# Norm totals from three matmuls, and ACT work moved inside a recurrence: one change to a five-engine transformer kernel

## The chip, the cores and the metric

One Trainium2 chip, one of its cores. The time is device microseconds of one execution. Before the change three runs took 2352.44, 2352.53 and 2354.01 us; their median is 2352.53 us. The engines are named as in the profile: PE (TensorE: matmuls and transposes, into PSUM), PEld (its weight loads), ACT (ScalarE), DVE (VectorE), POOL (GpSimd) and SP (SyncE, which issues the DMAs here).

## The reference

The kernel computes two transformer blocks on 512 tokens of width 1024, all in fp32. The first block has two layers, each an attention and an FFN with a short convolution; the second mixes a window attention, a global attention and a two-way gated recurrence over 64-wide heads, merges the three through sigmoid gates, and ends in an FFN and a norm. What the change touches is the norm, the recurrence's inputs and the merge:

```
def rmsnorm(x, g):
    y = x32 * lax.rsqrt(jnp.mean(x32 * x32, axis=-1, keepdims=True) + RMS_EPS)
    return (y * g)                       # before each attention and FFN
# second block, features of the recurrence: q and g pass through silu
# merge: sum over the three branches of sigmoid(gate) * (branch @ w_branch), then @ w_out
```

## The kernel before

**Layout.** x is held transposed in SBUF, 8 tiles `XT` of 128 features by 512 tokens. Features lie on partitions, so the mean of squares over features is a sum over partitions and over tiles.

**Weights.** Every 128 output columns of a weight matrix are a unit. Its weights come by DMA into `raw`; ACT copies them as fp32r, their high part, into `wH` (L460); DVE subtracts and leaves the low part in `wL` (L465). PE then does three matmuls for each 128 input features: high by high (L478), low by high (L479), high by low (L480), 512 tokens each. A ring of three `raw`, `wH` and `wL` buffers lets the conversion of a unit run ahead of PE; the conversion three units ahead is queued behind the eviction of the unit now done.

**Order of work.** There are five programs, one for each engine, and each is a fixed list. Signals (semaphores) tie them. An engine that waits holds up all that stands behind it on its list.

**Norm totals.** For a norm ACT squares tile k into `sq[k % 2]` (tile 0 straight into `ssum`; `ac_square`, L520), and one lane adds it to `ssum` (`add_square`, L527): DVE in the first attention ("attn0"), POOL in all others ("attn1", "ffn0", "ffn1", "ctx", "end1"). When all eight are in, PE multiplies `ssum` by a matrix of ones in plain fp32 (`pe_total`, L531, into PSUM bank 7), which sums over partitions, and ACT makes the factor with Ln and Exp (`ac_scale`). After the FFN of layer 1 two norms are needed at once, that of the block's end and the next block's; the second works on squares with a gain, `ssum_g`, and its own bank 6 (`pe_end_sums`, `pe_last_sums`). There the POOL sum runs to tile 6, and tile 7 comes in by a second matmul on each bank.

**The recurrence.** `g_order` (L2273) writes one list of items, and each engine's program takes from it what is its own. "ticks" are steps of the projection units that fill PE between the recurrence's own matmuls; their results are evicted by ACT (L2384), and the next gate's unit may wait for that. For each of four heads the items d (DVE, L2716 and L2718) and x (ACT, L2660) make the decay factors, w the products (DVE, L2730), use the score matmuls (PE, L2591), cp the masking (DVE, L2745), out the head's output. yh and yl split the branch outputs into high and low parts (`ac_split` on ACT, L2471, and `ve_split` on DVE, L2475) for the merge. silu is two Silu activations on ACT between two table loads (L2614 to L2617).

**The merge.** For each of 24 pairs of tile and branch, PE multiplies the branch output by its weights, ACT has a sigmoid of the gate ready (`ac_sigmoid`, L2482), DVE multiplies the two (L2878). In the order of the merge, ACT and DVE also do the last four splits (8 to 11).

Of the kernel before, what the change touches and what calls it, by code (L numbers as in the profile page):

```python
# [148 lines left out]
def build_in(nc, t, out, ctx):  # L149
# [551 lines left out]
    def ve_begin(ve):  # L701
# [11 lines left out]
        for k in range(1, KD):  # L713
            add_square(ve, ss_v, "attn0", k, S)
# [167 lines left out]
    def ve_fill(ve, layer):  # L882
        for x in fill[layer]:
# [15 lines left out]
            elif x.kind in ("q", "k"):  # L899
# [11 lines left out]
                if layer and x.kind == "k" and x.u == 1:  # L911
                    ve_factor(ve, 1)
# [615 lines left out]
    def pe_ffn(pe, layer):  # L1528
# [5 lines left out]
        for half in range(2):  # L1534
            for j in range(HALF):
                n = half * HALF + j
                for what, u, b in (("v", n, j % 2), ("g", 22 + n, 2 + j % 2)):
# [94 lines left out]
    def ac_ffn(ac, layer):  # L1632
# [18 lines left out]
        for half in range(2):  # L1651
# [40 lines left out]
            for m in range(8):  # L1692
# [8 lines left out]
                if half == 1:  # L1701
                    ac.wait_ge(*x_s.at(((down, 1), m)))
                    if layer == 1:
# [26 lines left out]
    def ve_ffn(ve, layer, scale=None):  # L1730
# [3 lines left out]
        if layer < 2:  # L1734
            ffn_free(ve, layer)
            if layer == 1:
                ve.do.tensor_tensor(sc1[:, 57:58], M("final", 7, 8), M("final", 7, 8), ALU.mult).then_inc(*gain_e.up(0))
                ve.wait_ge(*gain_e.at(0))
                ve.do.tensor_scalar(sc1[:, 57:58], sc1[:, 57:58], EPS, None, ALU.add).then_inc(*gain_e.up(1))
# [156 lines left out]
    def ffn1_done(lane):  # L1896
# [376 lines left out]
    def g_order():  # L2273

        out_ = [("ticks", 0, 2), ("sc", 0, 0), ("fa", 0, 1), ("fb", 0, 0), ("ticks", 0, 2), ("fv", 0, 1), ("sc", 0, 1),
                ("silu", 0), ("ke", 0, 0), ("kd", 0, 0), ("fb", 0, 1), ("ke", 0, 1), ("kd", 0, 1), ("ticks", 0, 4), ("v6", 0),
                ("ticks", 0, 99)]
        for h in range(4):
# [15 lines left out]
            out_ += [("use", h, 1), ("cp", h, 0), ("d", h, 4), ("w", h, 3), ("state", h, 1), *split(0), ticks_(3, 3), ("x", h, 4), ticks_(1, 1)]  # L2294
            out_ += [("use", h, 2), ("cp", h, 1), ("w", h, 4), ("d", h, 5), ("qe", h), *split(1), ticks_(1, 3), ("x", h, 5), ticks_(1, 1)]
            out_ += [("use", h, 3), ("cp", h, 2), ("w", h, 5), ("d", h, 6), *split(2), ticks_(2, 3), ("x", h, 6), ticks_(1, 1)]
            out_ += [("use", h, 4), ("cp", h, 3), ("w", h, 6), ("d", h, 7), ("qa", h), *split(3), ticks_(2, 3), ("x", h, 7), ticks_(1, 1)]
            out_ += [("use", h, 5), ("cp", h, 4), ("w", h, 7), *opens(("fa", 0)), *split(4), ticks_(2, 4)]
            out_ += [("use", h, 6), ("cp", h, 5), *opens(("fv", 0), ("fa", 1), ("sc", 0)), ticks_(3, 3)]
            out_ += [("use", h, 7), ("cp", h, 6), *opens(("fb", 0), ("ke", 0), ("kd", 0)), *split(5), ticks_(2, 2), ("cp", h, 7), ticks_(1, 1)]  # L2300
            out_ += [*opens(("fv", 1)), ("out", h), ("o", h), *opens(("sc", 1)), *split(6, 7), ticks_(3, 2)]
# [905 lines left out]
```

## Time and profile before

| | |
|---|---|
| median of three runs | 2352.53 us |
| the profiled execution | 2354.01 us |
| its span (first to last instruction) | 2352.2 us |
| PE busy | 2321.8 us (99%) |
| PEld busy | 1866.4 us (79%) |
| DVE busy | 1422.9 us (60%) |
| ACT busy | 1088.8 us (46%) |
| POOL busy | 407.4 us (17%) |
| fp32 sum matmuls L531 | 5 |
| POOL additions of squares L527, mean | 1470 ns |

The busy share of an engine is a mean over the whole span. In a timeline a row starts at its first number; the second is its length, and starts of consecutive matmuls stand closer than their lengths, because they are pipelined. Idle time before an instruction, where the profile shows it, stands in brackets with what ended it.

### The profile page before, as it was taken

The numbers are of one execution on the slowest core, as the hardware profiler recorded it, in microseconds if no ns is written. First come the engines' busy times: TensorE is split into PE (matmuls) and PEld (weight loads), VectorE is DVE, ScalarE is ACT, GpSimd is POOL, SyncE is SP. The second block draws the span as 40 slices with busy tenths as digits, with TensorE's granted clock in tenths as the row PEclk, the third lists the DMA queues.
The fourth block names the chain that finished last, engine by engine and source line by source line (L and its number), as shares of the span: only waits on it lengthen the run. The fifth ranks groups of instructions, "written<-read, shape, count | busy, mean of one in ns | idle before, by whom it ended". The sixth has DMA issues, their size and how long they took to land.

```text
span 2352.2 us, 30161 instructions
## 1 busy us (share of the span) xinstructions
PE 2321.8 (99%) x11870; PEld 1866.4 (79%) x11870; DVE 1422.9 (60%) x2280; ACT 1088.8 (46%) x1772; POOL 407.4 (17%) x304
## 2 busy tenths in 40 slices
PE   9999999999999999999999999999999999999998
PEld 7567678888887777888888878778887889888887
DVE  5887568858654546674676475557777335543443
ACT  4455654424435445442444356675555324432442
POOL 0001322202210001221122130012222222220222
PEclk9999999999999999999999999999999999999999
DMA  5222143433423222444342221011111432232331
GB/s 178 65 88 77 54 157 130 153 120 126 145 88 108 73 68 94 170 157 136 102 161 99 92 83 69 16 48 55 54 50 45 134 117 85 99 110 87 99 110 61
DMA packets 69933, 233.03 MB, mean 99 GB/s; under 512 B 8000, under 2 KB 10176, under 8 KB 69536
## 3 DMA queue, kind: packets, MB, share of 16 engines
q1 hardware_dynamic: 69792, 231.11, 29.3%
q8 instruction: 94, 1.54, 0.3%
q14 instruction: 47, 0.39, 0.0%
HBM read 224.18 MB, written 4.28 MB: 97 GB/s over the span
## 4 chain that ended last, share of the span: by engine, by line
PE 63%; DVE 4%; ACT 2%; issue 1%; DMA 0%; POOL 0%; DVEq 0%; SPq 0%; ACTq 0%
PE psum L478 17%; PE psum L479 17%; PE psum L480 17%; PE psum L1097 1%; PE psum L1122 1%; PE psum L1141 1%; PE psum L2011 1%; PE psum L2012 1%; PE psum L2013 1%; PE psum L1272 1%; PE psum L1283 1%; PE psum L1295 1%; DVE wL L465 1%; PE psum L2591 1%; DVE X L2716 0%
## 5 line engine op out<-in xcount | busy, mean ns | idle before, releaser
L478 PE MATMUL psum<-hH,wH 128*128 128x512 f32 (+1 forms) x1904 | 765.5, 402 | 11.5 <-ACT zc L2400 3.3
L480 PE MATMUL psum<-hH,wL 128*128 128x512 f32 (+1 forms) x1904 | 741.8, 390 | 0.0
L479 PE MATMUL psum<-hL,wH 128*128 128x512 f32 (+1 forms) x1904 | 740.6, 389 | 0.0
L465 DVE TENSOR_TENSOR wL<-raw,wH 128x1024 fp32r<-128x1024 f32 (+2 forms) x353 | 447.5, 1268 | 358.0 <-ACT wH L460 356.2
L460 ACT ACTIVATE wH<-raw 128x1024 fp32r<-128x1024 f32 (+2 forms) x353 | 363.3, 1030 | 481.1 <-PE psum L480 479.7
L478 PEld LDWEIGHTS psum<-hH,wH 128*128 128x128 f32 x1904 | 358.7, 188 | 115.8 <-issue 37.8
L480 PEld LDWEIGHTS psum<-hH,wL 128*128 128x128 f32 x1904 | 358.5, 188 | 75.0
L479 PEld LDWEIGHTS psum<-hL,wH 128*128 128x128 f32 x1904 | 359.3, 189 | 62.4 <-issue 0.7
L1845 POOL TENSOR_TENSOR sg<-sg,cv 128x512 f32<-128x512 f32 x66 | 95.1, 1441 | 676.9 <-ACT sg L1674 676.9
L478 PE MATMUL psum<-gH,wH 128*128 128x512 f32 x506 | 197.5, 390 | 0.0
L480 PE MATMUL psum<-gH,wL 128*128 128x512 f32 x506 | 196.9, 389 | 0.0
L479 PE MATMUL psum<-gL,wH 128*128 128x512 f32 x506 | 196.8, 389 | 0.0
L527 POOL TENSOR_TENSOR ssum<-ssum,sq 128x512 f32<-128x512 f32 (+1 forms) x44 | 64.7, 1470 | 401.3 <-ACT sq L520 400.2
L1310 ACT ACTIVATE Pr<-Sp,mn 128x128 f32<-128x128 f32 (+3 forms) x128 | 70.9, 555 | 101.4 <-DVE mn L1347 101.3
L1446 DVE TENSOR_TENSOR XT<-psum,XT 128x512 f32<-128x512 f32 x64 | 44.1, 689 | 118.3 <-PE psum L480 118.3
L478 PEld LDWEIGHTS psum<-gH,wH 128*128 128x128 f32 x506 | 95.0, 188 | 20.0 <-issue 0.2
L479 PEld LDWEIGHTS psum<-gL,wH 128*128 128x128 f32 x506 | 95.0, 188 | 19.8 <-issue 0.2
L480 PEld LDWEIGHTS psum<-gH,wL 128*128 128x128 f32 x506 | 95.0, 188 | 19.8
L1674 ACT ACTIVATE sg<-cg 128x512 f32<-128x512 f32 x66 | 41.8, 633 | 132.7 <-DVE cg L1772 132.7
L1847 POOL TENSOR_TENSOR gL<-sg,gH 128x512 fp32r<-128x512 f32 x66 | 87.9, 1332 | 49.0 <-ACT gH L1678 49.0
L1678 ACT ACTIVATE gH<-sg 128x512 fp32r<-128x512 f32 x66 | 41.7, 632 | 102.8 <-POOL sg L1845 102.8
L1763 DVE TENSOR_TENSOR hf<-psum,rs 128x512 f32<-128x512 f32 x88 | 60.5, 687 | 41.8 <-PE psum L480 25.9
(379 smaller groups left out, 3357.8 us busy)
## 6 DMA issues: line engine op xcount, KB each, us to landing
raw<-in_up SPq DMA_DIRECT2D x132, 512.0 KB, 3.6
raw<-in_dn SPq DMA_DIRECT2D x48, 704.0 KB, 4.0
raw<-in_win SPq DMA_DIRECT2D x56, 512.0 KB, 3.6
mbuf<-in_wmod SPq DMA_DIRECT2D x48, 512.0 KB, 3.7
raw<-in_we SPq DMA_DIRECT2D x33, 512.0 KB, 3.7
raw<-in_wq SPq DMA_DIRECT2D x24, 512.0 KB, 3.6
tm<-toep SPq DMA_DIRECT2D x32, 256.0 KB, 4.3
raw<-in_wo SPq DMA_DIRECT2D x32, 256.0 KB, 2.6
```

The source lines that it names most:

```text
L460: ac.do.activation(flat_of(wHb, n), flat_of(rawb, n), ACT.Copy).then_inc(*w_hi.up(n))
L465: ve.do.tensor_tensor(flat_of(wLb, n), flat_of(rawb, n), flat_of(wHb, n).bitcast(F), ALU.subtract).then_inc(*w_lo.up(n))
L478: pe.do.matmul(o, H[:, k, :], high(k), start=k == 0, stop=False)
L479: pe.do.matmul(o, H[:, k, :], low(k), start=False, stop=False)
L480: ins = pe.do.matmul(o, L[:, k, :], high(k), start=False, stop=k == kt - 1)
L527: lane.do.tensor_tensor(ssum[:, :n], ssum[:, :n], sq[k % 2][:, :n], ALU.add).then_inc(*own.up((z, k)))
L1310: ac.do.activation(Pr[:, s % 2, u, :W], Sp[:, u, :W], ACT.Exp, scale=-1.0, bias=mn[:, h:h + 1, i], accum_out=den[:, h:h + 1, i]).then_inc( ...
L1446: ve.do.tensor_tensor(xt(m), b, xt(m), ALU.add).then_inc(*x_s.up((key, m)))
L1674: ac.do.activation(sg[q][:], cg_[q][:], ACT.Silu).then_inc(*sg_a.up((layer, n)))
L1763: ve.do.tensor_tensor(of_[:], bank[b], rs[:], ALU.mult).then_inc(*up_s.up((layer, n, what)))
L1845: po.do.tensor_tensor(sg[q][:], sg[q][:], cv[q][:], ALU.mult).then_inc(*sg_p.up((layer, n)))
L1847: po.do.tensor_tensor(gL[:, j, :], sg[q][:], gH[:, j, :].bitcast(F), ALU.subtract).then_inc(*gl_s.up((layer, half, j)))
```

## The change

**Norm sums.** The additions of squares stop at tile 5. PE's total is now three fp32 matmuls that accumulate in bank 7: of `ssum`, of `sq[0]` (tile 6) and of `sq[1]` (tile 7). POOL does nine additions fewer (two each in ffn0, attn1, ffn1 and ctx, one in end1), DVE two fewer (attn0). The total of ffn0 and of ffn1 moves ahead by one unit, that of attn1 by six matmuls.

```
     def pe_total(pe, z, n):
-        pe.wait_ge(*(ss_v if z == "attn0" else ss_p).at((z, KD - 1)))
-        pe.do.matmul(bank[7][:, :n], C("ones"), ssum[:, :n], start=True, stop=True).then_inc(*tot.up(z))
+        pe.wait_ge(*(ss_v if z == "attn0" else ss_p).at((z, 5)))
+        pe.do.matmul(bank[7][:, :n], C("ones"), ssum[:, :n], start=True, stop=False)
+        pe.wait_ge(*sq_s.at((z, 6)))
+        pe.do.matmul(bank[7][:, :n], C("ones"), sq[0][:, :n], start=False, stop=False)
+        pe.wait_ge(*sq_s.at((z, 7)))
+        pe.do.matmul(bank[7][:, :n], C("ones"), sq[1][:, :n], start=False, stop=True).then_inc(*tot.up(z))
...
-                if i == 1 and layer and x.u == 1:
+                if i == 7 and layer and x.u == 0:
                     pe_total(pe, "attn1", S)
-                if i == 2 and layer and x.u == 2:
+                if i == 7 and layer and x.u == 1:
                     pe_factor(pe, 1)
...
-        last = {"ffn2": 5, "final": 5, "end1": 6}.get(z, KD - 1)
-        if 1 <= m <= last:
+        if 1 <= m <= 5:
             add_square(po, ss_p, z, m, n)
...
-                    if layer < 2 and n == 0 and what == "g":
+                    if layer < 2 and n == 0 and what == "v":
                         pe_total(pe, z, S)
```

In PE's list at ffn0 the total stands, before, between the unit on `wH_57` and that on `wH_55` (`cn` holds the ones):

```order
L478 MATMUL psum<-hH,wH_57 128x512
L479 MATMUL psum<-hL,wH_57 128x512
L480 MATMUL psum<-hH,wL_60 128x512
L478 MATMUL psum<-hH,wH_57 128x512
L479 MATMUL psum<-hL,wH_57 128x512
L480 MATMUL psum<-hH,wL_60 128x512
L531 MATMUL psum<-ssum,cn 128x512
L478 MATMUL psum<-hH,wH_55 128x512
```

and in the changed kernel:

```order
L478 MATMUL psum<-hH,wH_56 128x512
L479 MATMUL psum<-hL,wH_56 128x512
L480 MATMUL psum<-hH,wL_59 128x512
L478 MATMUL psum<-hH,wH_56 128x512
L479 MATMUL psum<-hL,wH_56 128x512
L480 MATMUL psum<-hH,wL_59 128x512
L531 MATMUL psum<-ssum,cn 128x512
L533 MATMUL psum<-sq_65,cn 128x512
L535 MATMUL psum<-sq_66,cn 128x512
L478 MATMUL psum<-hH,wH_57 128x512
```

One instruction has become three, and they stand one unit of 24 matmuls earlier, ahead of the unit on `wH_57`.

**End of the first block.** One matmul more on each bank, one DVE operation replaced by another, and two squares on ACT for tile 7, one of them scaled by the root of epsilon into a new buffer `sq_eps`:

```
         pe.wait_ge(*rs_ln.at("ctx"))
-        pe.wait_ge(*ss_p.at(("end1", 6)))
+        pe.wait_ge(*ss_p.at(("end1", 5)))
         pe.do.matmul(bank[7], C("ones"), ssum[:], start=True, stop=False)
+        pe.wait_ge(*sq_s.at(("end1", 6)))
+        pe.do.matmul(bank[7], C("ones"), sq[0][:], start=False, stop=False)
         pe.wait_ge(*x_s.at((("dn1", 1), 5)))
-        pe.wait_ge(*sgv.at("sum"))
+        pe.wait_ge(*sgv.at("eps"))
         pe.do.matmul(bank[6], C("ones"), ssum_g[:], start=True, stop=False)
 
     def pe_last_sums(pe):
-        pe.wait_ge(*sgv.at("last"))
-        pe.do.matmul(bank[6], C("ones"), hf[0][:], start=False, stop=True).then_inc(*rr_mm.up(0))
+        pe.wait_ge(*sg2.at(7))
+        pe.do.matmul(bank[6], C("ones"), hf[0][:], start=False, stop=False)
+        pe.wait_ge(*sg2.at("eps"))
+        pe.do.matmul(bank[6], C("ones"), sq_eps[:], start=False, stop=True).then_inc(*rr_mm.up(0))
...
-                elif half == 1 and layer == 1 and m == 7:
-
-                    ve.wait_ge(*x_s.at(((down, 1), 7)))
-                    ve.wait_ge(*gain_e.at(1))
-                    ve.do.scalar_tensor_tensor(hf[0][:], xt(7), sc1[:, 57:58], xt(7), ALU.mult, ALU.mult).then_inc(*sgv.up("last"))
+                    ve.wait_ge(*sgv.at("sum"))
+                    ve.wait_ge(*sq_s.at(("end1", 6)))
+                    ve.do.scalar_tensor_tensor(ssum_g[:], sq[0][:], EPS, ssum_g[:], ALU.mult, ALU.add).then_inc(*sgv.up("eps"))
```

**The opening of the recurrence.** The item ("silu", 0) moves behind the two key items and four ticks. ACT's list right behind the conversion into `wH_57`, before (`kd`, `kcc` and `f` are key products and decays; `XT<-psum` is the eviction of a gate's unit):

```order
L2615 ACT_TABLE_LOAD
L2615 ACTIVATE qt_129<-qt_129 128x512
L2616 ACTIVATE yc<-yc 128x512
L2617 ACT_TABLE_LOAD
L2537 ACTIVATE kd_152<-PS 128x256
L2541 ACTIVATE kd_152<-PS 128x128 x3
L2544 ACTIVATE f_147<-PS 128x4
L2528 ACTIVATE kcc<-t_1_150 128x768
L2537 ACTIVATE kd_146<-PS 128x256
L2541 ACTIVATE kd_146<-PS 128x128 x3
L2544 ACTIVATE f_147<-PS 128x4
L2384 ACTIVATE XT<-psum 128x512
```

and in the changed kernel:

```order
L2545 ACTIVATE kd_153<-PS 128x256
L2549 ACTIVATE kd_153<-PS 128x128 x3
L2552 ACTIVATE f_148<-PS 128x4
L2536 ACTIVATE kcc<-t_1_151 128x768
L2545 ACTIVATE kd_147<-PS 128x256
L2549 ACTIVATE kd_147<-PS 128x128 x3
L2552 ACTIVATE f_148<-PS 128x4
L2623 ACT_TABLE_LOAD
L2623 ACTIVATE qt_130<-qt_130 128x512
L2624 ACTIVATE yc<-yc 128x512
L2625 ACT_TABLE_LOAD
L2392 ACTIVATE XT<-psum 128x512
```

The two loads and the two activations now stand behind the last `f`, directly ahead of an eviction.

**Head 3.** The splits of yh and yl come earlier, and seven sigmoids move from the merge into head 3 between a pair of table loads. Splits by item, before: 0 after use 1, 1 after use 2, 2 after use 3, 3 after use 4, 4 after use 5, 5 after use 7, 6 and 7 after the head's output, 8 to 11 in the merge. Now:

```
+            out_ += [("use", h, 1), ("cp", h, 0), ("d", h, 4), ("w", h, 3), ("state", h, 1), *split(0, 1), ticks_(3, 3), ("x", h, 4), ticks_(1, 1)]
+            out_ += [("use", h, 2), ("cp", h, 1), ("w", h, 4), ("d", h, 5), ("qe", h), *split(2), ticks_(1, 3), ("x", h, 5), ticks_(1, 1)]
+            out_ += [("use", h, 3), ("cp", h, 2), ("w", h, 5), ("d", h, 6), *split(3, 4), ticks_(2, 3), ("x", h, 6), ticks_(1, 1)]
+            out_ += [("use", h, 4), ("cp", h, 3), ("w", h, 6), ("d", h, 7), ("qa", h), *split(5, 6), ticks_(2, 3), ("x", h, 7), ticks_(1, 1)]
+            out_ += [("use", h, 5), ("cp", h, 4), ("w", h, 7), *opens(("fa", 0)), *split(7), ticks_(2, 4)]
+            out_ += [("use", h, 6), ("cp", h, 5), *opens(("fv", 0), ("fa", 1), ("sc", 0)), *sigmoids(0, 2), ticks_(3, 3)]
+            out_ += [("use", h, 7), ("cp", h, 6), *opens(("fb", 0), ("ke", 0), ("kd", 0)), *sigmoids(2, 4), ticks_(2, 2), ("cp", h, 7), *split(8, 9, 10), *sigmoids(4, 7), ticks_(1, 1)]
```

The merge keeps split 11 and the sigmoids from 7 on. DVE's list in head 3 from the factors of d 6 to cp 4, before:

```order
L2716 TENSOR_TENSOR hf_pair<-PS 128x2x8x32
L2718 TENSOR_TENSOR hf_pair<-PS 128x2x8x32
L2475 TENSOR_TENSOR yL<-mixed_124,yH_164 128x512
L2745 COPY_PREDICATED ssum<-lmask,psum 128x512
L2730 TENSOR_TENSOR hf_pair<-hf_pair,qt_153 128x512
L2716 TENSOR_TENSOR X_155<-PS 128x2x4x64
L2718 TENSOR_TENSOR X_155<-PS 128x2x4x64
L2707 TENSOR_TENSOR sq_pair<-sq_pair,qt_153 128x1024
L2475 TENSOR_TENSOR yL<-mixed_124,yH_164 128x512
L465 TENSOR_TENSOR wL_59<-raw_53,wH_56 128x512
L2745 COPY_PREDICATED ssum<-lmask,psum 128x512
```

and in the changed kernel, for the same stretch:

```order
L2732 TENSOR_TENSOR hf_pair<-PS 128x2x8x32
L2734 TENSOR_TENSOR hf_pair<-PS 128x2x8x32
L2483 TENSOR_TENSOR yL<-mixed_125,yH_165 128x512
L2483 TENSOR_TENSOR yL<-mixed_125,yH_166 128x512
L2761 COPY_PREDICATED ssum<-lmask,psum 128x512
L2746 TENSOR_TENSOR hf_pair<-hf_pair,qt_154 128x512
L2732 TENSOR_TENSOR X_156<-PS 128x2x4x64
L2734 TENSOR_TENSOR X_156<-PS 128x2x4x64
L2723 TENSOR_TENSOR sq_pair<-sq_pair,qt_154 128x1024
L2483 TENSOR_TENSOR yL<-mixed_125,yH_166 128x512 x2
L465 TENSOR_TENSOR wL_59<-raw_53,wH_56 128x512
L2761 COPY_PREDICATED ssum<-lmask,psum 128x512
```

On the same stretch there are now four splits (`yL`) where there were two. One more stands ahead of the piece, where two follow the state update instead of one.

## Rows read from the trace of the kernel before

**Rows 1.** the page, its part 1: busy us (share of span) and instructions of each engine.

```profile
PE 2321.8 (99%) x11870; PEld 1866.4 (79%) x11870; DVE 1422.9 (60%) x2280; ACT 1088.8 (46%) x1772; POOL 407.4 (17%) x304
```

**Rows 2.** the waits of PE, whole span: what it waited for, us, times, longest.

```profile
PE psum L478 <- ACT zc L2400: 3.3, 3, 1.4
PE psum L478 <- ACT hcG L2384: 3.0, 2, 2.1
```

**Rows 3.** timeline of PE at ffn0's total: start us, us, instruction, [idle before <- releaser].

```profile
339.64 0.39 PE L480 MATMUL psum<-hH,wL 128*128 128x512 f32 x1
339.86 1.02 PE L531 MATMUL psum<-ssum,cn 128*128 128x512 f32 x2
...
340.95 0.39 PE L479 MATMUL psum<-hL,wH 128*128 128x512 f32 x1
```

**Rows 4.** timeline of PE at the context's total (256 columns).

```profile
1095.22 0.59 PE L531 MATMUL psum<-ssum,cn 128*128 128x256 f32 x2
...
1095.88 0.39 PE L479 MATMUL psum<-gL,wH 128*128 128x512 f32 x1
```

**Rows 5.** timeline of PE at attn0's total.

```profile
20.85 0.34 PE L480 MATMUL psum<-hH,wL 128*128 128x384 f32 x1
21.88 1.10 PE L531 MATMUL psum<-ssum,cn 128*128 128x512 f32 x2 [0.69 <-DVE ssum L527]
22.91 0.61 PE L683 MATMUL psum<-oh,rel 32*32 32x512 f32 x1
```

**Rows 6.** timeline of all engines in layer 1's first unit.

```profile
691.17 1.30 POOL L527 TENSOR_TENSOR ssum<-ssum,sq 128x512 f32<-128x512 f32 x1 [4.81 <-ACT sq L520]
...
692.08 1.47 DVE L465 TENSOR_TENSOR wL<-raw,wH 128x1024 fp32r<-128x1024 f32 x1 [2.26 <-ACT wH L460]
...
694.27 0.50 PE L478 MATMUL psum<-hH,wH 128*128 128x512 f32 x1 [0.42 <-DVE hL L632]
```

**Rows 7.** timeline of all engines at the opening of the recurrence.

```profile
1570.92 1.28 ACT L2615 ACT_TABLE_LOAD   x1
1570.94 1.23 DVE L465 TENSOR_TENSOR wL<-raw,wH 128x1024 fp32r<-128x1024 f32 x1 [1.81 <-ACT wH L460]
...
1574.06 2.11 DVE L2512 TENSOR_TENSOR_SCAN PS<-cn,PS 128x256 f32<-128x256 f32 x4
...
1574.68 0.51 ACT L2537 ACTIVATE kd<-PS 128x256 f32<-128x256 f32 x1
...
1576.82 0.49 ACT L2537 ACTIVATE kd<-PS 128x256 f32<-128x256 f32 x1
...
1578.19 0.58 ACT L2384 ACTIVATE XT<-psum 128x512 f32<-128x512 f32 x1
...
1580.94 0.60 ACT L2384 ACTIVATE XT<-psum 128x512 f32<-128x512 f32 x1 [1.22 <-PE psum L480]
...
1581.75 0.47 PE L478 MATMUL psum<-hH,wH 128*128 128x512 f32 x1
```

**Rows 8.** windows: us, busy us of each engine (instructions), granted clock, DMA.

```profile
1729.00:1733.00 4.00, 2.66 (x17) 2.21 (x16) 3.57 (x4) 3.94 (x6) 1.28 (x1) 1.00 0.00 0
1772.00:1797.00 25.00, 21.33 (x107) 17.37 (x106) 24.71 (x35) 11.80 (x17) 8.04 (x5) 0.93 0.12 35
1777.80:1780.80 3.00, 3.00 (x8) 2.32 (x7) 3.00 (x6) 1.48 (x3) 0.00 (x0) 0.50 0.00 0
```

**Rows 9.** timeline of all engines in head 3 of the recurrence.

```profile
1774.14 0.68 DVE L2718 TENSOR_TENSOR X<-PS 128x512 f32<-128x512 f32 x1
...
1776.50 0.50 PE L478 MATMUL psum<-hH,wH 128*128 128x512 f32 x1 [2.05 <-ACT hcG L2384]
...
1780.21 0.68 DVE L2475 TENSOR_TENSOR yL<-mixed,yH 128x512 fp32r<-128x512 f32 x1
...
1786.63 0.50 PE L478 MATMUL psum<-hH,wH 128*128 128x512 f32 x1 [0.96 <-ACT hcG L2384]
```

**Rows 10.** timeline of PE in the merge.

```profile
1809.56 0.39 PE L480 MATMUL psum<-yH,wL 128*128 128x512 f32 x1
1810.05 0.50 PE L478 MATMUL psum<-yH,wH 128*128 128x512 f32 x1
```

More of the change, by code:

```diff
@@ L244, in build_in @@
     ctxT = sb("ctxT", [128, KD, CTX], at=ctx_at)
+    sq_eps = sb("sq_eps", [128, S], at=ctx_at)
     top[0] = ctx_at + 8192
@@ L712, in ve_begin @@
             ve_low(ve, n)
-        for k in range(1, KD):
+        for k in range(1, 6):
             add_square(ve, ss_v, "attn0", k, S)
@@ L910, in ve_fill @@
                     ve.do.tensor_tensor(kT[:, x.c % 3, :], x.bank, rs[:], ALU.mult).then_inc(*ev_v.up(x.n))
-                if layer and x.kind == "k" and x.u == 1:
+                if layer and x.u == 1:
                     ve_factor(ve, 1)
@@ L1708, in ac_ffn @@
                             ac.do.activation(ssum_g[:], xt(m), ACT.Square, scale=gain).then_inc(*sg2.up(m))
-                        elif m < 7:
+                        else:
                             if m == 1:
@@ L1714, in ac_ffn @@
                             ac.do.activation(hf[0][:], xt(m), ACT.Square, scale=gain).then_inc(*sg2.up(m))
+                        if m == 7:
+                            ac.wait_ge(*hl_v.at(("ctx", 7)))
+                            ac.do.activation(sq_eps[:], xt(m), ACT.Square, scale=math.sqrt(EPS)).then_inc(*sg2.up("eps"))
                     if m == 0:
@@ L1735, in ve_ffn @@
             ffn_free(ve, layer)
[L1736 to L1739, printed above, removed]
             ve.wait_ge(*rs_s.at(z))
@@ L1899, in ffn1_done @@
         lane.wait_ge(*sq_s.at(("end1", 7)))
-        lane.wait_ge(*ss_p.at(("end1", 6)))
+        lane.wait_ge(*ss_p.at(("end1", 5)))
         lane.wait_ge(*sgv.at(6))
@@ L2275, in g_order @@
         out_ = [("ticks", 0, 2), ("sc", 0, 0), ("fa", 0, 1), ("fb", 0, 0), ("ticks", 0, 2), ("fv", 0, 1), ("sc", 0, 1),
-                ("silu", 0), ("ke", 0, 0), ("kd", 0, 0), ("fb", 0, 1), ("ke", 0, 1), ("kd", 0, 1), ("ticks", 0, 4), ("v6", 0),
+                ("ke", 0, 0), ("kd", 0, 0), ("fb", 0, 1), ("ke", 0, 1), ("kd", 0, 1), ("ticks", 0, 4), ("silu", 0), ("v6", 0),
                 ("ticks", 0, 99)]
@@ L2284, in split, with sigmoids @@
                 return [(x, c) for c in cs for x in ("yh", "yl")] if h == 3 else []
+            def sigmoids(a, b):
+                return [("sigmoids", a, b)] if h == 3 else []
             def opens(*xs):
@@ L2293, in g_order @@
             out_ += [("use", h, 0), ("d", h, 3), ("w", h, 2), ticks_(1, 2), ("x", h, 3), ticks_(1, 1)]
[L2294 to L2301, printed above, removed]
+            out_ += [("use", h, 1), ("cp", h, 0), ("d", h, 4), ("w", h, 3), ("state", h, 1), *split(0, 1), ticks_(3, 3), ("x", h, 4), ticks_(1, 1)]
[5 more added lines that the diff above has]
+            out_ += [("use", h, 7), ("cp", h, 6), *opens(("fb", 0), ("ke", 0), ("kd", 0)), *sigmoids(2, 4), ticks_(2, 2), ("cp", h, 7), *split(8, 9, 10), *sigmoids(4, 7), ticks_(1, 1)]
+            out_ += [*opens(("fv", 1)), ("out", h), ("o", h), *opens(("sc", 1)), ticks_(3, 2)]
             out_ += [*opens(("fb", 1), ("ke", 1), ("kd", 1)), ticks_(1, 0)]
@@ L2630, in ac_recurrence @@
                     ac.wait_ge(*gemm.at(at["win", 27]))
-                else:
+                elif h < 8:
                     ac.wait_ge(*g_fv.at((3, 1, 1)))
                     ac.wait_ge(*t6_mm.at(("h", 3)))
+                else:
+                    ac.wait_ge(*g_kv.at((3, 1)))
+                    ac.wait_ge(*g_tz.at(h - 8))
                 ac_split(ac, h)
+            elif what == "sigmoids":
+                for n in range(h, d):
+                    ac_sigmoid(ac, n)
+                if d == 7:
+                    ac.do.preload_act_table_set("natural_log_exp_and_others")
             elif what == "o":
@@ L2825, in ac_merge @@
             z = n % 2
+            if n == 2:
+                ac.wait_ge(*g_tz.at(3))
+                ac_split(ac, 11)
             if n >= N_EARLY:
@@ L2831, in ac_merge @@
                 ac.do.activation(gt[z][:], bank[z], ACT.Sigmoid).then_inc(*m_g.up((m, br)))
-            else:
+            elif n >= 7:
                 ac_sigmoid(ac, n)
-            if n == 2:
-                ac.wait_ge(*g_tz.at(3))
-                ac_split(ac, 11)
             ac_high(ac, at["wbr", 8 * br + m] + 3)
-            if n < 2:
-                for c in ((8,), (9, 10))[n]:
-                    ac_split(ac, c)
             if n >= 2 and MERGE[n - 2][1] == 2:
@@ L2861, in ve_merge @@
             z = n % 2
+            if n == 3:
+                ve_split(ve, 11)
             if n >= N_EARLY:
```

6 lines of the change are left out of this document (1 added, 5 removed).

## The prediction

> **What bounds the kernel now.** The page's first part comes first. PE is busy for 2321.8 of 2352.2 us, 99% of the span, and no other engine passes 60% [rows 1]. So nearly every microsecond of PE work that is added is a microsecond of time, and a wait counts only where PE itself stands still. The second view is the list of PE's waits: all that PE stands idle comes to 2352.2 − 2321.8 = 30.4 us, spread over more than a dozen places. The change can reach few of these: the gate evictions in the recurrence (3.0 us, two of them [rows 2]), the total of attn0 (0.69 [rows 5]), and one wait for hL in layer 1 (0.42 [rows 6]). The third view is the timeline around each edited place, which tells what PE does there and what comes last. The reader is to see that the extra matmuls fall on an engine without slack, while the additions that go lie on POOL and DVE, where few were waited for.
>
> **Norm sums: what is added.** One fp32 matmul by ones is recorded as two passes. At ffn0 it starts at 339.86; the low-high matmul after the next one starts at 340.95. Matmuls of 512 columns otherwise follow each other 0.22 to 0.23 us apart (339.64 to 339.86). Without the total, that second matmul would have started one step after 339.86, so the total costs 340.95 − 0.23 − 339.86 = 0.86 us [rows 3]. With 256 columns it costs 1095.88 − 0.23 − 1095.22 = 0.43 us [rows 4]. PE does not wait ahead of either. The two added matmuls are of the same form and shape, so I price them the same.
>
> - ffn0, ffn1, attn1: two each at 0.86 us, 1.72 us each, 5.16 together.
> - ctx: two at 0.43, 0.86 us.
> - end1: one on bank 7 and one on bank 6, 1.72 us.
> - attn0: two, 1.72 us, against the wait that goes. There PE stops after the matmul at 20.85 and reaches the total at 21.88, where it had waited 0.69 us on DVE's additions. The total and what follows end up at 22.91 [rows 5]. The squares of tiles 6 and 7 are ready by then, since two additions follow the last square, so three totals can start at about 21.03 and fill 2.56 us, to 23.6. Net +0.7.
>
> Sum: 5.16 + 0.86 + 1.72 + 0.7 = 8.4 us.
>
> **Norm sums: what goes.** Nine POOL additions (mean 1.47 us) and two DVE ones come off. None is waited for at ffn0 or ctx, where PE arrives without an idle gap [rows 3, 4]. The moves ahead in PE's list (24 matmuls, or 24 × 0.227 = 5.45 us, in the FFNs; six in attn1) fetch nothing: PE had no wait at the totals, and the squares are then ready too. At attn1 there is one small gain. PE waits 0.42 us at 694.27 for hL, which follows on DVE the conversion at 692.08; that takes 1.47 us beside a POOL addition that begins at 691.17 and lasts 1.30 [rows 6], while a conversion of the same shape takes 1.23 us elsewhere [rows 7]. The addition falls away, so 0.24 us of the wait goes. Bounds: 0 to 0.42. At end1 the extra DVE operation replaces another of its size, and both new squares on ACT have a matmul unit to hide in; cost nothing, up to 0.6 us if ACT is late for the last matmul. Norm sums together: 8.4 − 0.24 = +8.2 us, bounds 7.8 to 9.0.
>
> The Trainium skill, "SBUF — State Buffer", § Who interferes with whom, has it that DVE and GpSimd share one pair of SBUF ports, held exclusively by whichever has it. By that rule the two rows of conversions (1.47 beside POOL, 1.23 without) differ for this reason; the rule gives the same 0.24 us and speaks against putting more two-input splits on DVE in head 3, where POOL is active too.
>
> **The silu item.** The block of load, two activations and load runs from 1570.92 to the next key product at 1574.68, 3.76 us [rows 7]. Moving it behind the last f leaves the keys of step 1 bound by DVE's scan, which ends at about 1574.06 + 2.11 = 1576.2; what ACT does behind it took 1578.19 − 1576.82 = 1.37 us, so the last f ends at about 1577.6 rather than 1578.19 [rows 7]. Then comes the silu block, to about 1581.4, and only then the eviction of gate 2 (1578.19 before), its conversion (0.5 and 1.05 us), and the eviction of gate 3: at about 1583.0, where it was at 1580.94 [rows 7]. Gate 4's unit on PE starts at 1581.75, right behind the transposes, and needs gate 3's bank. It will start at about 1583.6. PE's added wait: 1583.6 − 1581.75 = 1.85 us. Behind the late eviction on ACT stand a conversion for a unit two later and the copies of kdT; the latter feed the state products some 5 us on, and PE arrives there 1.85 us later as well, so no second wait. Bounds: 0, if gate 3's bank isn't what is late, or the eviction's consumer has slack I don't see; 2.65 (1583.0 + 0.6 against 1580.94) if the kdT copies come fully late too. I take 1.85, the row itself.
>
> **Head 3.** DVE is busy 24.71 of 25.00 us from 1772 to 1797 [rows 8], so what is put there delays all behind it. A split is 0.60 us on DVE (start to start; 0.68 long [rows 9]). Up to cp 4 there are seven splits where four stood, 3 × 0.60 = 1.8 us. The path there: DVE's factors release ACT's x, this the gate's eviction, this PE's next gate unit: PE idles 2.05 us before 1776.50 and 0.96 before 1786.63 [rows 9]. The first wait has no added split ahead and stays; the second has two, and the wait for cp 4 has three. Some of the 1.8 us is slack in operations stretched beside POOL, so I take +1.3; bounds 0.6 and 1.8. In the merge the splits 8 to 10 and the first sigmoids are gone from ACT and DVE; the step from 1809.56 to 1810.05, 0.49 us where 0.23 is the pace [rows 10], loses its 0.26. The new table loads and sigmoids lie where ACT has idle time while PE and DVE finish the head; cost nothing, up to 0.5 if they delay the head's last square. Net +1.0 us, bounds −0.3 to +2.3.
>
> **Sum.** 8.2 + 1.85 + 1.0 = 11.05 us on the profiled execution, 2354.01 → 2365.1. That execution was 1.48 us over the median of the three, so a median of 2363.6 us, +0.47%.
>
> **Rivals.** I call no change what lies within 0.2% (4.7 us: 2347.8 to 2357.2), about what a measurement of this kernel can tell.
>
> 1. *The clock falls after a new gap.* In head 3, after 2.05 us of idleness, PE's granted clock reads 0.50 (1.2 of 2.4 GHz) from 1777.80 to 1780.80; after a wait of 1.4 us for zc, the longest of three [rows 2], the window 1729 to 1733 around it stays at 1.00 [rows 8]. Seven matmuls at half rate lose 7 × 0.23, about 1.5 us. The new gap of 1.85 and the widened one of about 1.8 (0.96 + the splits) lie between these two cases. One such fall gives 2365.1, both 2366.6. For it: the gaps are nearer to 2.05 than to 1.4. Against: the transposes just before are PE work too. 25% for at least one.
> 2. *Silu or splits cost nothing.* If the eviction of gate 3 isn't what the unit waits for, and the splits fill gaps, what stays is 8.2 us or a little more: 2352.5 + 8.2 = 2360.7. For it: only 0.8 us lie between that eviction and its user before. 15%.
> 3. *Not slower: head 3's waits vanish.* If the new order lets DVE reach the factors ahead of both gates earlier, gone are 2.05 + 0.96 us of wait, the 1.5 us at half clock, and in the merge 0.26: 4.8 us, and with a silu move that costs nothing 8.2 − 4.8 = +3.4, 2355.9 us, no change. It decides at DVE: it must come to the first factors 2 us sooner. Against: nothing is taken off DVE ahead of them. 7%. That the whole change is faster would need the added matmuls to be free, for which no row speaks: 2%.
> 4. *Table loads cost more than their rows.* A switch might hold ACT longer than the load is recorded. The row shows 1.28 us and the next activation 0.02 us behind it, so the extra is nil; were it about as long again, the silu block and PE's gap would be unchanged (both loads only move), and the added pair in head 3 would be 2.6 us longer and delay the head's square by up to 2.5 us: 2366.1. 2%. The Trainium skill, "ScalarE: Activation LUTs", § What ACT_TABLE_LOAD costs, gives about 1283 ns for the load and about 1380 ns more to drain, 2.66 us for each switch; the trace agrees with the first figure and shows nothing of the second.
>
> **How the numbers follow.** Forecast 49%, 2362 to 2365; rival 1 25%, rival 2 15%, rival 3 7 + 2%, rival 4 2%. Bounds of the terms: low 7.8 + 0 − 0.3 = +7.5, 2360.0; high 9.0 + 2.65 + 2.3 = +13.95, 2366.5, with clock losses more. I set 2357.5 to 2368.0: it holds all but rival 3 and the rarest sums. Slower by over 0.2%: 0.90; within 0.2%: 0.08; faster: 0.02.
>
> **What would show it.** Three rows of fp32 passes at each total, 0.86 us apart on PE without idle time; at attn0 no wait for DVE; at the opening of the recurrence a wait of L478 for the gate's eviction near 1.85 us; in head 3 the wait of 0.96 grown and that of 2.05 as before; PE busy some 9 us more. The prediction is wrong if PE's busy time hardly grows, if the silu gap is missing, or if the waits in head 3 shrink.

## The result, and the profile after

The changed kernel took 2365.28 us (median of six runs, 2363.68 to 2369.0), the kernel before 2353.44 us in the runs beside it: a ratio of 1.0052, 95% interval 1.0039 to 1.0065. It is 11.8 us slower, at a forecast of +11.05. A few executions of the kernels here, of 2566 to 6231 us, were disturbed by something that no row shows; the ratios and their intervals leave them out.

Part 1 of the page, the changed kernel:

```profile
PE 2328.2 (98%) x11894; PEld 1868.6 (79%) x11894; DVE 1419.2 (60%) x2276; ACT 1092.8 (46%) x1776; POOL 395.6 (17%) x295
```

Against [rows 1] PE's busy time grew by 6.4 us and the span by 11.5, so about 5 us are new waits. PE's waits (what it waited for, us, times, longest):

```profile
PE psum L478 <- ACT hcG L2392: 4.7, 2, 2.7
...
PE psum L478 <- ACT zc L2408: 3.3, 3, 1.4
PE psum L478 <- ACT XT L2392: 2.7, 1, 2.7
...
PE psum L2599 <- DVE ssum L2761: 1.6, 3, 0.8
```

Against [rows 2] the wait for hcG has grown from 3.0 to 4.7 us, that for zc is the same, and a wait for the eviction into `XT` (2.7 us) is new. The wait for attn0's additions is gone. Laying the two traces over each other on PE, matmul by matmul, shows where the shift between them (start of a matmul in the changed kernel less its start in the kernel before) changes:

| place | change of the shift, us | forecast |
|---|---|---|
| attn0's total | +0.8 | +0.7 |
| layer 1, hL wait before attn1's total | −0.3 | −0.24 |
| ffn0, attn1, ffn1 totals | +1.7 each | +1.72 each |
| context total | +0.8 | +0.86 |
| end1, both banks | +1.7 | +1.72 |
| gate 4's unit at the opening | +3.0 | +1.85 |
| head 3 (−1.6 where a half-clock stretch of before is missing, then +2.9 in waits) | +1.3 | +1.3 |
| merge | −0.4 | −0.26 |

A half-clock stretch is one in which the granted clock of PE reads 0.50, as in [rows 8]. The remainder, some −0.6, lies ahead of attn0's total, where before has such a stretch and the changed kernel has none, and behind it. The timeline of PE at attn1's total, changed kernel (start us, us, instruction, idle before):

```profile
696.24 0.39 PE L480 MATMUL psum<-hH,wL 128*128 128x512 f32 x1
696.48 1.02 PE L531 MATMUL psum<-ssum,cn 128*128 128x512 f32 x2
697.33 1.02 PE L533 MATMUL psum<-sq,cn 128*128 128x512 f32 x2
698.19 1.02 PE L535 MATMUL psum<-sq,cn 128*128 128x512 f32 x2
...
699.28 0.39 PE L479 MATMUL psum<-hL,wH 128*128 128x512 f32 x1
```

The three totals start 0.85 and 0.86 us apart with no idle bracket, and the second matmul of the next unit comes 1.09 us after the last total's start, as at 340.95 in [rows 3]. In the first unit of layer 1 PE's wait for hL is 0.17 us instead of 0.42, behind a conversion that no POOL addition stands beside and that takes 1.23 us instead of 1.47 [rows 6]:

```profile
693.73 1.23 DVE L465 TENSOR_TENSOR wL<-raw,wH 128x1024 fp32r<-128x1024 f32 x1 [2.26 <-ACT wH L460]
```

At attn0:

```profile
20.60 0.34 PE L480 MATMUL psum<-hH,wL 128*128 128x384 f32 x1
20.78 1.02 PE L531 MATMUL psum<-ssum,cn 128*128 128x512 f32 x2
21.64 1.02 PE L533 MATMUL psum<-sq,cn 128*128 128x512 f32 x2
22.49 1.02 PE L535 MATMUL psum<-sq,cn 128*128 128x512 f32 x2
23.45 0.61 PE L687 MATMUL psum<-oh,rel 32*32 32x512 f32 x1
```

The wait of 0.69 us [rows 5] is gone; 2.67 us of totals stand in its place.

The opening of the recurrence, all engines, changed kernel:

```profile
1580.09 1.20 POOL L2773 TENSOR_TENSOR kd<-kd,kcc 128x256 f32<-128x256 f32 x1 [149.88 <-ACT f L2552]
...
1580.72 1.38 DVE L2512 TENSOR_TENSOR t<-PS,zc 128x768 f32<-128x768 f32 x1
...
1582.13 2.81 DVE L2520 TENSOR_TENSOR_SCAN PS<-cn,PS 128x256 f32<-128x256 f32 x4
...
1586.27 0.20 ACT L2552 ACTIVATE f<-PS 128x4 f32<-128x4 f32 x1
...
1590.24 0.60 ACT L2392 ACTIVATE XT<-psum 128x512 f32<-128x512 f32 x1
...
1591.68 0.59 ACT L2392 ACTIVATE XT<-psum 128x512 f32<-128x512 f32 x1
...
1592.32 0.50 PE L478 MATMUL psum<-hH,wH 128*128 128x512 f32 x1 [2.68 <-ACT XT L2392]
```

The second eviction starts at 1591.68 and PE after it, 2.68 us idle. Head 3, PE:

```profile
1787.12 0.50 PE L478 MATMUL psum<-hH,wH 128*128 128x512 f32 x1 [2.05 <-ACT hcG L2392]
...
1794.04 1.13 PE L2599 MATMUL psum<-X 128*128 128x128 f32 x8 [0.27 <-DVE ssum L2761]
1797.83 0.50 PE L478 MATMUL psum<-hH,wH 128*128 128x512 f32 x1 [2.66 <-ACT hcG L2392]
...
1805.23 1.02 PE L2599 MATMUL psum<-hf_pair 128*128 128x128 f32 x7 [0.76 <-DVE ssum L2761]
```

The first wait for hcG is 2.05 as in [rows 9], the second has gone from 0.96 to 2.66. Two more maskings are waited for than before: masking 2 for 0.27 us and masking 4 for 0.76 us (maskings are counted from 0).

### The profile page after: what moved, and what is told of

The parts are those of the page before. It is cut to its first block, busy times and chain, and to the rows that moved or that the text cites. A ratio compares the mean times of both kernels' runs of the same rounds, so it can differ in the third digit from the quotient of the medians.

```text
span 2363.7 us, 30192 instructions
## 1 busy us (share of the span) xinstructions
PE 2328.2 (98%) x11894; PEld 1868.6 (79%) x11894; DVE 1419.2 (60%) x2276; ACT 1092.8 (46%) x1776; POOL 395.6 (17%) x295
## 4 chain that ended last, share of the span: by engine, by line
PE 63%; DVE 4%; ACT 2%; issue 1%; DMA 0%; POOL 0%; DVEq 0%; SPq 0%; ACTq 0%
PE psum L478 17%; PE psum L480 17%; PE psum L479 17%; PE psum L1101 1%; PE psum L1126 1%; PE psum L1145 1%; PE psum L2016 1%; PE psum L2017 1%; PE psum L2018 1%; PE psum L1276 1%; PE psum L1287 1%; PE psum L1299 1%; DVE wL L465 1%; PE psum L2599 0%; DVE X L2732 0%
## 5 line engine op out<-in xcount | busy, mean ns | idle before, releaser
L527 POOL TENSOR_TENSOR ssum<-ssum,sq 128x512 f32<-128x512 f32 (+1 forms) x35 | 52.3, 1495 | 393.5 <-ACT sq L520 392.9
```

Of the source, the lines that this page charges most:

```text
L527: lane.do.tensor_tensor(ssum[:, :n], ssum[:, :n], sq[k % 2][:, :n], ALU.add).then_inc(*own.up((z, k)))
```

## The experiments

Eight kernels, each the kernel before with one or two edits. Times are medians beside runs of before on the same chip (2353.39 us for the first four, 2353.21 for the others).

### The norm sums alone (e1_sums)

The edit is the change's first two parts as they are: the totals of three matmuls, their places, and the end of the first block.

```
+        pe.do.matmul(bank[7][:, :n], C("ones"), sq[0][:, :n], start=False, stop=False)
...
+        pe.do.matmul(bank[7][:, :n], C("ones"), sq[1][:, :n], start=False, stop=True).then_inc(*tot.up(z))
```

> The norm-sum part of the change alone (all totals and end1), silu item and head 3 as before. My theory: each added fp32 matmul on PE costs its own 0.86 us (0.43 for 256 columns), since PE has no slack at the totals. Expected +8.2 us over before (7.8 to 9.0), PE busy about 9 us more, the shift between the traces made of steps of 0.86 us per added matmul. Rival: the cost of the sums comes from moved waits, then the steps would differ from multiples of 0.86 us and idle brackets would stand at the totals. Second rival: part of the 11.8 us is an interaction of the parts, then this kernel and the two others here do not add up to it.

Measured: 2361.50 us, +8.1, ratio 1.0034 (1.0021 to 1.0046). The shifts on PE are those of the table above, place by place. No idle bracket stands at a total. The first rival falls: the price is that of the matmuls. The second, an interaction of the parts, is taken up under "Do the parts add up?" below. PE's busy time on the page:

```profile
PE 2329.5 (99%) x11894; PEld 1869.5 (79%) x11894; DVE 1419.3 (60%) x2276; ACT 1090.5 (46%) x1774; POOL 396.3 (17%) x295
```

That is 7.7 us more than before, though this profile has one half-clock stretch fewer, at its start.

### The silu item alone (e2_silu)

```
-                ("silu", 0), ("ke", 0, 0), ("kd", 0, 0), ("fb", 0, 1), ("ke", 0, 1), ("kd", 0, 1), ("ticks", 0, 4), ("v6", 0),
+                ("ke", 0, 0), ("kd", 0, 0), ("fb", 0, 1), ("ke", 0, 1), ("kd", 0, 1), ("ticks", 0, 4), ("silu", 0), ("v6", 0),
```

> The silu item moved alone. My theory: PE waits once, for ACT's eviction of gate 3, by about 2.7 us (as in the changed kernel), and the time rises by 2.3 to 3.1 us. My prediction had 1.85. Theory for the difference: POOL's two key products of step 0 now run beside DVE's last operation and its scan and stretch them (scan 2.8 instead of 2.1 us), so ACT's keys of step 1 come late; then the scan in this kernel is long as well. Rival: the wait in the changed kernel depends on the other edits (another phase of the units); then the gap here is near 1.85 and the scan 2.1 us.

Measured: 2357.79 us, +4.4, ratio 1.0020 (1.0010 to 1.0029), more than the 2.3 to 3.1 expected. The gap is as expected; what I had not put into the number is what followed it. Timeline, all engines:

```profile
1571.96 1.20 POOL L2757 TENSOR_TENSOR kd<-kd,kcc 128x256 f32<-128x256 f32 x1 [149.89 <-ACT f L2544]
...
1572.60 1.38 DVE L2504 TENSOR_TENSOR t<-PS,zc 128x768 f32<-128x768 f32 x1
...
1574.01 2.81 DVE L2512 TENSOR_TENSOR_SCAN PS<-cn,PS 128x256 f32<-128x256 f32 x4
...
1578.14 0.20 ACT L2544 ACTIVATE f<-PS 128x4 f32<-128x4 f32 x1
...
1584.20 0.79 PE L478 MATMUL psum<-hH,wH 128*128 128x512 f32 x1 [2.68 <-ACT XT L2384]
```

and the window behind the gap (us, busy of PE, PEld, DVE, ACT, POOL, granted clock, DMA):

```profile
1584.20:1587.20 3.00, 3.00 (x7) 2.42 (x8) 2.79 (x5) 1.03 (x2) 0.00 (x0) 0.50 0.42 126
```

PE waits 2.68 us, which shifts it by 2.9 us, then runs 3 us at 0.50 of its clock, which shifts it by 1.4 us more. The runs of this kernel lie in two groups, three at 2354.9 to 2355.2 and six from 2357.6 to 2359.0, with one at 2365.2. The three of the first group read a mean granted clock of 0.999 over the whole execution, the six of the second 0.997 or 0.998. Runs of the kernel before, beside them, that read 0.999 took 2351.8 to 2352.2 us, so at equal clock the move costs some 3.0 us, what the trace shows without the half-clock stretch.

### The same with POOL held back (e4_silu_pool)

```
                 po.wait_ge(*g_fe.at((h, d, 0)))
+                if h == 0 and d == 0:
+                    po.wait_ge(*g_sc.at((0, 1, 3)))
```

> The silu item moved alone, and in addition POOL's key product of head 0, step 0 waits for the end of DVE's scan of step 1. My theory (contention of POOL and DVE): scan back to about 2.1 us and the operation ahead of it to 0.96, the last f about 1.1 us earlier, PE's wait about 1.6 us where the silu move alone has 2.7, and the time about 1.1 us below that kernel. Rival (DVE's operations are long for another reason): scan and wait unchanged within 0.2 us.

Measured: 2355.30 us, +1.9, ratio 1.0009 (0.9999 to 1.0019), 2.5 us below the silu move alone. Timeline, all engines:

```profile
1571.42 0.96 DVE L2504 TENSOR_TENSOR t<-PS,zc 128x768 f32<-128x768 f32 x1
...
1572.41 2.11 DVE L2512 TENSOR_TENSOR_SCAN PS<-cn,PS 128x256 f32<-128x256 f32 x4
...
1574.69 0.74 POOL L2759 TENSOR_TENSOR kd<-kd,kcc 128x256 f32<-128x256 f32 x1 [153.75 <-DVE PS L2512]
...
1575.85 0.19 ACT L2544 ACTIVATE f<-PS 128x4 f32<-128x4 f32 x1
...
1581.91 0.50 PE L478 MATMUL psum<-hH,wH 128*128 128x512 f32 x1 [1.55 <-ACT XT L2384]
```

With POOL behind the scan, the operation ahead of it takes 0.96 us, not 1.38, and the scan 2.11, not 2.81. PE's wait falls from 2.68 to 1.55 us, by the 1.1 us of the forecast. So the part of the silu gap that the prediction missed is contention between POOL and DVE. The time fell by more than the 1.1 us expected; no half-clock stretch follows the wait in this profile, which would account for 1.4 us, but the intervals of the two kernels overlap and don't show the difference.

### Head 3 and the merge alone (e3_head3)

The edit is the change's last part: earlier splits, seven sigmoids moved.

```
-            ... *split(0) ... *split(1) ... *split(2) ... *split(3) ... *split(4) ... *split(5) ... *split(6, 7)
+            ... *split(0, 1) ... *split(2) ... *split(3, 4) ... *split(5, 6) ... *split(7) ... *split(8, 9, 10)
```

> The head 3 and merge part alone (earlier splits, sigmoids moved). My theory: the splits on the busy DVE widen the wait for the gate's eviction from 0.96 to about 2.7 us and the waits for the masking by about 1 us, 2.7 us in all; the merge gives 0.3 back. If the half-clock stretch of before (1.5 us after the 2.05 us gap) is caused by this order of work and goes with it, the sum is +0.9; if it comes and goes with the phase of the execution, it is +0.9 without such a stretch and +2.4 with one.

Measured: 2354.94 us, +1.5, ratio 1.0007 (0.9997 to 1.0016), which the runs don't tell apart from none. The mechanism is read from the trace, where head 3 costs 2.2 us and the merge gives 0.4 back. PE's timeline:

```profile
1775.88 0.50 PE L478 MATMUL psum<-hH,wH 128*128 128x512 f32 x1 [2.06 <-ACT hcG L2387]
...
1782.81 1.13 PE L2594 MATMUL psum<-X 128*128 128x128 f32 x8 [0.28 <-DVE ssum L2756]
1786.59 0.50 PE L478 MATMUL psum<-hH,wH 128*128 128x512 f32 x1 [2.65 <-ACT hcG L2387]
```

The second gate wait is 2.65 us as in the changed kernel. Here the clock did not halve after the first gap but did after the second, which shifts PE by 1.6 us. The wait for masking 4, 0.76 us in the changed kernel, is absent here: the loss took its place. Head 3 costs 2.2 us with this stretch and 1.3 us without it in the changed kernel, so 0.9 of the 1.6 us remain. Time that PE loses in front of a wait for DVE is free only up to the length of that wait.

### Evictions ahead of x in head 3 (e5_evict)

```
-            ... *split(0), ticks_(3, 3), ("x", h, 4), ticks_(1, 1)]
+            ... *split(0), ticks_(3, 4), ("x", h, 4), ticks_(1, 0)]
-            ... *split(2), ticks_(2, 3), ("x", h, 6), ticks_(1, 1)]
+            ... *split(2), ticks_(2, 4), ("x", h, 6), ticks_(1, 0)]
```

> The kernel before with one edit in head 3 on ACT alone: the two evictions of a gate's bank (hcG) stand ahead of the item x instead of behind it. It asks which engine bounds head 3. My theory: DVE, busy 24.7 of 25 us there. PE's two waits for hcG (2.05 and 0.96 us) vanish, but PE then waits for DVE's masking (ssum) by nearly as much; the end of head 3 moves by at most 0.3 us, plus 1.5 us where a half-clock stretch of before is gone or hidden. Time 0 to 1.8 us less. Rival: the eviction's place on ACT is the bound; then the waits go and are not given back, and the time falls by 3 us or more.

Measured: 2353.49 us, +0.3, ratio 1.0003 (0.9994 to 1.0012), no change that the runs can tell. PE's timeline:

```profile
1772.68 1.13 PE L2591 MATMUL psum<-X 128*128 128x128 f32 x8 [0.58 <-DVE ssum L2745]
...
1778.03 1.13 PE L2591 MATMUL psum<-hf_pair 128*128 128x128 f32 x8 [1.46 <-DVE ssum L2745]
...
1782.20 1.13 PE L2591 MATMUL psum<-X 128*128 128x128 f32 x8 [0.28 <-DVE ssum L2745]
...
1792.65 1.13 PE L2591 MATMUL psum<-hf_pair 128*128 128x128 f32 x8 [2.94 <-DVE ssum L2745]
```

No wait for hcG is left. PE waits for the masking instead, 1.46 and 2.94 us, and behind the wait for masking 4 it stands where it stood in the kernel before, to 0.1 us. DVE bounds head 3 up to there, and the gate waits that the prediction (and the changed kernel) made longer were only where that showed. Behind the 2.94 us this profile has a half-clock stretch (the second to last number), which costs 1.6 us:

```profile
1794.00:1797.00 3.00, 3.00 (x9) 2.33 (x8) 2.10 (x4) 0.00 (x0) 0.00 (x0) 0.50 0.35 94
```

### Splits later, alone (e7_late_only), and both (e6_late)

```
-            ... *split(0) ... *split(1) ... *split(2) ... *split(3) ... *split(4) ...
+            ... ("cp", h, 4), ("w", h, 7), ... *split(0), ticks_(2, 4)]
...
+            ... ("cp", h, 6), ... *split(1, 2), ticks_(2, 2), ("cp", h, 7), *split(3, 4, 5), ticks_(1, 1)]
```

> The kernel before with the opposite of the change's edit in head 3: the splits 0 to 5 come later (0 after use 5, 1 and 2 after masking 6, 3 to 5 after masking 7), so four splits (2.4 us of DVE) stand no more ahead of masking 4. My theory (each split ahead of a masking or factor delays PE by its 0.6 us): the wait of 0.96 goes, the wait for masking 4 goes, the first wait of 2.05 stays; 1.2 us less, up to 2.5 with a half-clock stretch gone. Rival (the waits of head 3 depend on ACT's order and not on DVE's load): within 0.3 us of before.

Measured: 2351.78 us, −1.4, ratio 0.9993 (0.9983 to 1.0002), which the runs don't tell apart from none. A half miss: masking 4 is done 1.6 us ahead of PE's use of it, where in the kernel before PE's use followed it by 0.15 us, but the second gate wait stays, at 1.07 us, where I had it vanish. PE reached it 1.6 us earlier, having lost no time at half clock, and the gate's eviction came 1.5 us earlier, with two splits fewer ahead of it: 0.96 + 1.6 − 1.5 = 1.1. In this profile head 3 is 1.8 us shorter, and 1.6 of that is the half-clock stretch of before that it does not have; the later splits alone gave PE next to nothing. PE's timeline:

```profile
1772.69 1.13 PE L2591 MATMUL psum<-X 128*128 128x128 f32 x8 [0.59 <-DVE ssum L2745]
1775.87 0.50 PE L478 MATMUL psum<-hH,wH 128*128 128x512 f32 x1 [2.06 <-ACT hcG L2384]
...
1784.51 0.50 PE L478 MATMUL psum<-hH,wH 128*128 128x512 f32 x1 [1.07 <-ACT hcG L2384]
```

With the evictions ahead of x as well:

> Both edits together: the evictions of the gate's bank ahead of x in head 3, and the splits 0 to 5 later. My theory: with DVE relieved of 2.4 us and ACT's eviction out of the way nothing holds PE in head 3 for more than a few tenths: 2.5 to 3.5 us less than before, and no gap over 2 us after which PE's clock can halve, another 0 to 1.5 us. Rival: the moved splits collide with the masking of column block 7 or the merge's first unit and give it back there; then an idle gap stands at the merge's first matmul and the time is that of before.

Measured: 2350.14 us, −3.1, ratio 0.9987 (0.9978 to 0.9996), its expectation. One wait is longer than the few tenths expected, that for masking 4. PE's timeline:

```profile
1773.09 1.13 PE L2591 MATMUL psum<-X 128*128 128x128 f32 x8 [0.59 <-DVE ssum L2745]
...
1777.32 1.13 PE L2591 MATMUL psum<-hf_pair 128*128 128x128 f32 x8 [0.36 <-DVE ssum L2745]
...
1789.92 1.13 PE L2591 MATMUL psum<-hf_pair 128*128 128x128 f32 x8 [1.37 <-DVE ssum L2745]
```

Neither edit alone gives this: with the evictions ahead DVE is the bound, with the splits later ACT's order is. DVE's own way through the head shows it, from the start of masking 0 to that of masking 4; in the changed kernel:

```profile
1783.07 0.72 DVE L2761 COPY_PREDICATED ssum<-lmask,psum 128x512 f32<-128x512 uint8 x1
...
1804.38 0.71 DVE L2761 COPY_PREDICATED ssum<-lmask,psum 128x512 f32<-128x512 uint8 x1
```

| kernel | splits on the way | masking 0 to masking 4, us | half-clock stretch of PE on the way |
|---|---|---|---|
| before | 4 | 20.03 | yes |
| evictions ahead of x | 4 | 19.98 | no |
| changed | 7 | 21.31 | no |
| head 3 and merge alone | 7 | 21.29 | yes |
| splits later | 0 | 16.83 | no |
| both | 0 | 16.84 | no |

The way depends on how many splits stand on it, and neither on the place of the evictions nor on PE's clock. Three splits more lengthen it by 1.3 us, not by 3 × 0.60 = 1.8: the two operations behind masking 3 on DVE, stretched beside a POOL product, take 2.33 us in the kernel before and 1.84 in the changed one. With both edits PE's head 3 is shorter by the same 3.2 us as DVE's way; with the splits later alone PE does not follow.

### Evictions ahead of x in heads 0 to 2 too (e8_all_evict)

```
-            ... ("qa", h), ticks_(2, 3), ("x", h, 7), ticks_(1, 1)]
+            ... ("qa", h), ticks_(3, 3), ("x", h, 7), ticks_(0, 1)]
```

> As the kernel with both edits of head 3, and in heads 0 to 2 the eviction of a finished projection unit (zc) ahead of the item x 7 on ACT. There PE waits 1.35 and 1.34 us and a shorter time for zc behind an x of 1.06 us. My theory: DVE has room in these heads, so these 3.3 us go nearly whole, 2.5 to 3.3 us below the kernel without this edit and 5 to 7 us below before. Rival: DVE's chain bounds these heads too; then PE waits for the masking instead, and the gain is under 1 us.

Measured: 2346.81 us, −6.4, ratio 0.9971 (0.9960 to 0.9981), 3.3 us below the kernel without this edit. PE's waits for the masking, 2.3 us with a longest of 1.4 without this edit, are now:

```profile
PE psum L2591 <- DVE ssum L2745: 2.3, 3, 1.3
```

The 3.3 us for zc are gone from the list of waits, and none for the masking came in their place; those heads were bound by ACT's order. This is the fastest kernel of the study, some 18 us under the changed one.

## Why the prediction was right

**The sum.** +11.05 was forecast and +11.8 measured, inside the range. That the total came so close is partly luck: the silu term was 1.1 us too small, 0.6 of that was offset between the two profiles by the start, and what the clock takes or leaves, up to 1.6 us for each half-clock stretch, is as large as the miss. The bulk, the norm sums, was right in size and mechanism: +8.2 forecast, +8.1 measured alone, and the steps in the trace are the price of one fp32 matmul on an engine with no slack. The −0.24 us by the POOL addition that goes came as −0.3.

**The silu item.** The mechanism was right (gate 3's eviction late, PE waits once), the size too small: 1.85 us forecast, 2.68 idle and 3.0 of shift. The step that failed is that moving the item "leaves the keys of step 1 bound by DVE's scan, which ends at about" 1576.2: I took the scan's 2.11 us from before. The first keys come 3.8 us earlier, so POOL's products fall on DVE's operations and stretch them, the scan from 2.11 to 2.81 us and the operation ahead of it from 0.96 to 1.38. The kernel with POOL held back gives 1.55 idle and 1.8 of shift, the value forecast. The prediction had used this contention at attn1 and not looked for it where the moved item brings POOL's work forward.

**Head 3.** Net +0.9 in the trace for +1.0 forecast: +1.3 for the splits, as forecast, and −0.4 in the merge where I had −0.26. The splits were miscounted at the second gate: the prediction has two more ahead of it, but in the item list only one (split 2) comes ahead of the factors of d 6, which release x 6 and the eviction behind it. The eviction came 0.60 us later in the changed kernel, one split. The +1.3 rests on masking 4, which has three more ahead and came 1.3 us later. How it is made up on PE I had not foreseen either. In before, PE ran at half clock behind the first gate wait [rows 8]; in this profile of the changed kernel it did not, and came 1.6 us earlier to waits that DVE sets. They were longer by that much and by the 1.3 us of the splits: 1.70 us at the second gate and about 1.2 at the maskings, 2.9 in all. So in the kernel before the clock's loss cost nothing up to masking 4: DVE's way there is 20.03 us with it and 19.98 without. My term of 1.5 us for such a stretch, in rivals 1 and 3, is right only where PE is the bound, as behind the silu gap (1.4 us); behind the second gate of head 3, 0.9 of 1.6 us remained.

**The rivals.** Rival 1, a clock fall after the new gap, was put as a matter of the gap's length. In the profile of the changed kernel both gaps are longer than 2.05 us and neither was followed by a fall; in that of the silu kernel the same gap of 2.68 was. What the other runs of the changed kernel did there no profile shows. Rival 2 did not come: gate 3's eviction was what the unit waited for, and the splits did not fill gaps. Nor did rival 3: for it DVE would have had to reach the factors sooner, and with three splits more its way is 1.3 us longer. Rival 4: the changed kernel has the load of 1.28 us with the next activation 0.02 us behind, and no further cost. "PE busy some 9 us more" was wrong by what the clock gives: 6.4, since time at half clock counts as busy and this profile has two such stretches fewer.

**Do the parts add up?** Alone they gave +8.1, +4.4 and +1.5, 14.0 in all, against 11.8 together. The difference of 2.2 us is within the intervals (each about ±2 to 3 us), so the times don't show an interaction and don't exclude one. Place by place the traces show none: the totals' steps are the same in the norm-sum kernel and the changed one, the silu gap is 2.68 us in both kernels that have it without the hold on POOL, and DVE's way through head 3 is 21.3 us in both. What differs is which gaps the clock fell after (one such stretch while PE worked in the changed kernel's profile, three in that of the silu kernel), and these are enough to make 2.2 us.

## What to carry to other kernels

On PE, 99% busy here, each added matmul cost its full time at every one of its places; to take additions off an engine that nobody waits for buys nothing for it. When a move makes a lane start earlier, look for what it then runs beside, and reprice that. When a wait names one engine, try which engine's load is behind it before moving work: here two edits that were each worth too little to measure gave 3.1 us together.

## What the runs showed of the hardware

**PE's clock after a gap.** In ten profiles (before, changed, eight experiments) PE stood still 32 times from one matmul's start to the next for 2.3 to 3.3 us, and 20 times a stretch of about 3 us at 1.2 GHz (0.50 of 2.4) began, between 0.4 us ahead of the gap's end and 1.5 us behind it, costing up to 1.6 us. After gaps of 1.3 to 1.9 us, five to nine in each profile, it came once: in the profile of the silu kernel, some 2 us behind this wait at attn0's total, where two matmuls start 1.45 us apart:

```profile
21.89 1.10 PE L531 MATMUL psum<-ssum,cn 128*128 128x512 f32 x2 [1.11 <-DVE ssum L527]
```

The first gate gap of head 3, 2.33 us in seven of the profiles, was followed by such a stretch in four and not in three. So the length alone does not settle it, and what does stays open. Runs of one and the same program differ as well: the kernel before read mean granted clocks from 0.996 (2356.03 us) to 0.999 (2351.76 us). Such a stretch in the changed kernel, behind the wait for `mixed` that it shares with before:

```profile
1376.40:1379.40 3.00, 3.00 (x8) 2.32 (x7) 2.93 (x4) 0.57 (x2) 0.45 (x1) 0.50 0.00 0
1797.80:1800.80 3.00, 2.97 (x14) 2.47 (x15) 3.00 (x5) 1.84 (x4) 0.85 (x1) 1.00 0.00 0
```

The first window is at 0.50, right behind a wait of 2.04 us, the second, right behind the 2.66 us wait of head 3, at 1.00.

**POOL beside DVE.** DVE's four scans took 2.81 us beside POOL's products and 2.11 without; the tensor-tensor operation ahead of them 1.38 and 0.96. The first POOL product beside them took 1.20 us, and 0.74 alone, the second 1.73 and 1.01: both engines lose. The Trainium skill, "SBUF — State Buffer", § Who interferes with whom, explains such a loss by one pair of SBUF ports that DVE and GpSimd share under an exclusive lock; by that rule the stretch of the two-input operation was to be expected, and the trace agrees with it: the 1.38 us against 0.96.
